# Summing part of the modulation on VectorE during the merge of the branches, in a two-layer hybrid backbone on one core

## The reference

```python
sh1, sc1, g1, sh2, sc2, g2 = split(silu_c @ w_mod[l] + b_mod[l], 6)   # c_ctx the same: csh1 ...
u = h * (1 + sc1) + sh1
p = u @ w_in[l]                       # conv, attention, mLSTM inputs, and 3 x 1024 branch gates
y = (sig(ga)*(ya @ w_a) + sig(gb)*(yb @ w_b) + sig(gc)*(yc @ w_c)) @ w_out
h = layer_norm(alpha*h + g1*y);  u2 = h * (1 + sc2) + sh2
h = layer_norm(alpha*h + g2*moe(u2))  # 16 experts, top 1 group, top 2 experts in it
```

## Time and profile before

| what | us |
| --- | --- |
| median of 3 runs (lowest, highest) | 1658.95 (1657.82, 1660.44) |
| the profiled execution, its own time | 1658.97 |
| its span, first to last instruction | 1657.1 |
| TensorE busy | 1561.0 (94%) |
| VectorE busy | 768.3 (46%) |
| ScalarE busy | 374.5 (23%) |
| GpSimd busy | 219.1 (13%) |
| transfers, mean | 220 GB/s |
| granted TensorE clock, mean | 0.981 of full |

### The profile page before, as it was taken

How to read it: one execution, slowest core, us unless ns; L and a number is a source line. 1 busy time by engine, 2 the same in 40 slices (tenths; PEclk the granted TensorE clock), 3 DMA queues, 4 the chain that set the end, 5 groups by cost and what they waited for, 6 DMA issues and landing times.

```text
span 1657.1 us, 32449 instructions
## 1 busy us (share of the span) xinstructions
PE 1561.0 (94%) x13532; PEld 981.8 (59%) x13532; DVE 768.3 (46%) x1543; ACT 374.5 (23%) x894; POOL 219.1 (13%) x239
## 2 busy tenths in 40 slices
PE   6999999999999999999999896999999998999974
PEld 3454475465444468656566454767688887555532
DVE  3169825475001023653336536395553125565455
ACT  1100036642000010422222122002742002212111
POOL 0200000000000000033334230000000000543421
PEclk9999999999999999999999997999999998999997
DMA  9534647602313242699669998452215467999993
GB/s 334 172 106 138 228 159 272 200 22 81 113 52 114 64 152 74 253 406 406 250 251 404 406 400 300 152 143 80 64 42 191 154 216 260 374 407 407 407 408 152
DMA packets 175107, 365.30 MB, mean 220 GB/s; under 512 B 14337, under 2 KB 93801, under 8 KB 174451
## 3 DMA queue, kind: packets, MB, share of 16 engines
q1 hardware_dynamic: 162400, 330.43, 54.9%
q0 software_dynamic: 10112, 27.06, 4.8%
q10 hardware_dynamic: 2451, 5.73, 1.1%
HBM read 356.66 MB, written 10.62 MB: 222 GB/s over the span
## 4 chain that ended last, share of the span: by engine, by line
PE 64%; DVE 5%; SPq 4%; DMA 3%; ACT 2%; issue 1%; POOL 0%; DVEq 0%; POOLq 0%; ACTq 0%
PE psum L1120 62%; SPq L930 4%; PE psum L1658 1%; DMA yab<-in_moe_w_gu 1%; DMA uT<-in_moe_w_gu 1%; PE psum L1410 0%; DMA convT<-us,x_row 0%; DMA yab<-ys 0%; PE psum L1228 0%; DMA ys<-qkT,y_row 0%; DVE st L2153 0%; DVE H L2725 0%; DVE st L2154 0%; DVE H L2166 0%; PE psum L1551 0%
## 5 line engine op out<-in xcount | busy, mean ns | idle before, releaser
L1120 PE MATMUL psum<-uT,ring 128*128 128x512 f32 (+1 forms) x1440 | 494.7, 501 | 2.9 <-ACT uT L1823 2.1
L1120 PEld LDWEIGHTS psum<-uT,ring 128*128 128x128 f32 x1440 | 272.9, 191 | 212.0 <-issue 192.3
L1120 PE MATMUL psum<-ring,mo_tok 128*32 128x256 f32 x4992 | 317.0, 382 | 20.3 <-DVE ring L2702 19.0
L1120 PEld LDWEIGHTS psum<-ring,mo_tok 128*32 128x32 f32 x4992 | 153.7, 110 | 129.9 <-DVE ring L2702 35.5
L1120 PE MATMUL psum<-ring,v_tok 128*32 128x256 f32 x2496 | 150.7, 382 | 0.5 <-ACT v_tok L2072 0.5
L2310 DVE SCALAR_TENSOR_TENSOR convT<-upad,cwT,convT 128x512 f32<-128x512 f32 (+1 forms) x240 | 132.4, 614 | 2.1
L1120 PEld LDWEIGHTS psum<-ring,v_tok 128*32 128x32 f32 x2496 | 82.2, 111 | 54.8 <-issue 1.8
L1120 PE MATMUL psum<-ring,uT 128*128 128x256 f32 (+1 forms) x576 | 113.6, 357 | 0.0
L1120 PEld LDWEIGHTS psum<-ring,uT 128*128 128x128 f32 x576 | 99.1, 190 | 16.6 <-issue 5.4
L2527 DVE TENSOR_TENSOR arena<-psum,mqk 128x512 f32<-128x512 f32 (+1 forms) x16 | 8.9, 558 | 206.2 <-PE psum L1120 206.2
L2702 DVE COPY ring<-uT 128x1024 f32<-128x1024 f32 x73 | 49.8, 728 | 83.8 <-PE psum L1120 76.0
(11 more groups left out here) (361 smaller groups left out, 1547.7 us busy)
## 6 DMA issues: line engine op xcount, KB each, us to landing
ring<-in_w_in SPq DMA_DIRECT2D x104, 512.0 KB, 4.8
ring<-in_w_mod SPq DMA_DIRECT2D x84, 512.0 KB, 7.3
yab<-in_moe_w_gu SPq DMA_DIRECT2D x51, 512.0 KB
arena<-in_moe_w_gu SPq DMA_DIRECT2D x47, 512.0 KB
uT<-in_moe_w_gu SPq DMA_DIRECT2D x47, 512.0 KB
mv_tok<-in_moe_w_gu SPq DMA_DIRECT2D x26, 512.0 KB
uT<-in_moe_w_dn SPq DMA_DIRECT2D x26, 512.0 KB
mqk<-in_moe_w_gu SPq DMA_DIRECT2D x25, 512.0 KB
```

The source lines that it names most:

```text
L1120: return nc.tensor.matmul(dst, lhsT, rhs, start=start, stop=stop)
```

## The change

The units of `w_mod` are grouped anew. Group 2 becomes six units of the first layer (twelve halves), which take the place of the old group 3 in the attention's steps; the eight spots behind mqk, mv and mo are gone. Groups 3, 4 and 5 become one group of 14 units, 28 halves: the two units of the first layer's last gate and all of the second layer. These are not multiplied on TensorE. VectorE multiplies each 128x512 piece of a half by the matching column of `cT` (one scalar for each partition) and adds it up in one of eight 128x512 buffers, one for each unit and stream: for six units both streams, for the other eight the latent stream alone, 20 sums. TensorE then only adds the 128 partitions, four sums at a time in the four column groups, with a stationary operand that is one column of ones (`add_partitions`).

In the stream, eight halves follow the weights of each pair of merge steps, four for each step, 28 in all; VectorE sums four halves after it has merged a step, and a slot is freed when its half is summed. The loads at the border, the wait on `mod_used` before the last gathers, and the column steps of the old groups 2, 4 and 5 fall away; the column step of the new group stands after the second output product. `cT` gets narrower (its width follows the largest group computed on TensorE).

```diff
+    [(0, u) for u in range(4, 10)],
+    [(0, 10), (0, 11)] + [(1, u) for u in range(12)],
 ]
+SUMMED = 3
+BOTH_STREAMS = [(0, 10), (0, 11)] + [(1, u) for u in range(4)]
+SUMS = [(x, c) for x in MOD_GROUPS[SUMMED] for c in range(2 if x in BOTH_STREAMS else 1)]
+SUM_BUFS = 8
+SUM_BATCH = 4
+HALVES_PER_MERGE = 4
+BATCH_AFTER_MERGE = {1: 0, 2: 1, 3: 2, 5: 3}
...
                 if c + l + 1 < KD // 2:
                     used_gates(c + l + 1)
+                for j in (2 * c, 2 * c + 1):
+                    used_sums(halves_at_merge(l, j))
...
+                def add_partitions(batch):
+
+                    sums = SUMS[SUM_BATCH * batch:SUM_BATCH * (batch + 1)]
+                    pe.wait_ge(summed, 2 * MOD_GROUPS[SUMMED].index(sums[-1][0]) + 2)
...
+                    for q, (x, c) in enumerate(sums):
+                        row = 2 * MOD_GROUPS[SUMMED].index(x) + c
+                        last = mm(psum[MOD_BANK][32 * q:32 * q + 32, :], one_column[:, 31 - row:63 - row],
+                                  sum_bufs[sum_of(x, c) % SUM_BUFS], batch == 0, batch == N_BATCHES - 1)
+                    last.then_inc(mod_used, 1)
...
                     if j + GATES_AHEAD[l] < KD:
                         branch_gates(j + GATES_AHEAD[l])
+                    if l == 0 and j in BATCH_AFTER_MERGE:
+                        add_partitions(BATCH_AFTER_MERGE[j])
...
+                    if key == out_keys(0)[0]:
+                        add_partitions(N_BATCHES - 1)
+                    if key == out_keys(0)[1]:
+                        modulation_columns(SUMMED)
...
-                    for t in range(2):
+                    for t in range(nt):
                         gather_tile(t)
                     act.wait_ge(rows_used, 2 * l + 2)
                     gate_rows(1)
-                    act.wait_ge(mod_used, halves_to(5))
-                    for t in range(2, nt):
-                        gather_tile(t)
-                    keep_rows(5)
...
+                def sum_half(x):
+
+                    m, u, half = x
+                    streams = [c for y, c in SUMS if y == (m, u)]
+                    wait_slot(dve, "mod", *x)
...
+                    for q in range(4):
+                        for c in streams:
+                            acc = sum_bufs[sum_of((m, u), c) % SUM_BUFS]
+                            w, scale = slot_wide(slot_of("mod", *x))[:, q, :], cT[:, 4 * half + q, MOD_AT + c:MOD_AT + c + 1]
+                            if (half, q) == (0, 0):
+                                last = v.tensor_scalar(acc, w, scale, None, ALU.mult)
+                            else:
+                                last = v.scalar_tensor_tensor(acc, w, scale, acc, ALU.mult, ALU.add)
+                        if q < 3:
+                            link(last)
+                    last.then_inc(summed, 1)
...
+                    for x in halves_at_merge(l, j):
+                        sum_half(x)
```

More of the change, by code:

```diff
@@ L103, in halves_to, with mod_uses, gate_group, halves_at_merge @@
     return sum(len(halves) for halves in MOD_HALVES[:g + 1])
[L106 to L125, removed]
+def mod_uses(g):
+    return halves_to(min(g, SUMMED - 1)) + (N_BATCHES if g == SUMMED else 0)
+def gate_group(layer, which):
+    return 2 if (layer, which) == (0, 0) else SUMMED
+MOD_STEPS = (1, 2, 3, 4, 5, 6, 7, 9, 11, 13, 15, 17)
+MOD_SPREAD = dict(zip(MOD_STEPS, MOD_HALVES[2]))
+assert len(MOD_STEPS) == len(MOD_HALVES[2])
+COLUMNS_UNIT = len(UNITS)
+def halves_at_merge(layer, j):
+    return MOD_HALVES[SUMMED][HALVES_PER_MERGE * j:HALVES_PER_MERGE * (j + 1)] if layer == 0 else []
+assert sum(len(halves_at_merge(0, j)) for j in range(KD)) == len(MOD_HALVES[SUMMED])
+def sum_of(x, c):
+    return SUMS.index((x, c))
 BRANCHES = ("bga", "bgb", "bgc")
@@ L581, in build @@
         sig = mqk
+        sum_bufs = [buf[:, x * 512:(x + 1) * 512] for buf in (ln_rows, convT[:, :, :].rearrange("p a b -> p (a b)"))
+                    for x in range(SUM_BUFS // 2)]
         spread_rows = [[qkT[:, 4, :], qkT[:, 5, :], upad_flat[:, 3 * T:4 * T]],
@@ L740, in used_modulation, with used_sums @@
                 stream.append((("mod",) + x, mod_used, MOD_ORDER.index(x) + 1))
-            def used_pair(pair):
-                for x in pair:
-                    used_modulation(x)
+            def used_sums(halves):
+                for x in halves:
+                    stream.append((("mod",) + x, summed, MOD_HALVES[SUMMED].index(x) + 1))
             def used_gates(c):
@@ L972, in _ @@
                     at += NS
-                    for x in range(len(BORDER) if l == 0 else 0):
-                        load_border(x)
                 else:
@@ L1414, in _ @@
                         outputs_of_group(i // 2 - 2)
-                    modulation_pair(mod_at(l, "step", i))
+                    if l == 0 and i in MOD_SPREAD:
+                        modulation(MOD_SPREAD[i])
                     spread_gates("step", i)
-                    if l == 0 and i == COLUMNS_STEP:
-                        modulation_columns(2)
                 pe.wait_ge(gate_em, l + 1)
@@ L1594, in _ @@
                 done(last, "count", l)
-                if l == 0:
-                    for x in MOD_HALVES[4][1:]:
-                        modulation(x)
                 def uses_until(key):
@@ L1748, in _ @@
                     gate_rows(1, G2)
-                    for x in BORDER:
-                        modulation(x)
                 else:
@@ L2560, in _ @@
                         norm_half(1, part)
+                    if key == out_keys(0)[1]:
+                        modulation(SUMMED)
+                        wait_drained(dve, "modt", SUMMED)
+                        for w in (2, 3):
+                            fold_norm(w)
                 modulate(1)
```

138 lines of the change are left out of this document (44 added, 94 removed).

## The result

The changed kernel took **1700.99 us** (median of 4 runs, 1697.62 to 1703.95), beside 1659.7 us for the kernel before: a ratio of 1.0258, 95% interval 1.0238 to 1.0277. Forecast were 1690 us and a range of 1674 to 1704. The profiled execution was the slowest of the four: 1703.95 us, span 1702.2 us, 45.1 us above the span before.

What follows compares the result with a forecast made beforehand. TensorE, busy for 94% of the span, was taken to bound the kernel. Gains of 21.7 us against losses of 52.8 us, net +31.1 on 1658.97 us, gave 1690 us; the range was 1674 to 1704 us.

Steps and rivals of the forecast that it cites:

- The gaps' place and cause: Merge stretch: TensorE idles after steps 1, 3 and 5, since the next a/b weights queue behind halves in the ring; 38.4 us.
- VectorE's own term: Sums on VectorE: 160 added operations, some 111 us, with VectorE's capacity not the problem.
- Their size: Merge stretch: three gaps of 12.8 us each, a batch of 1.0 us inside each, 38.4 us lost in all.
- At 30.9 us TensorE is ready for step 2: Merge, counted from step 1's start: a/b weights end a burst of eight transfers, 4.19 MB, 12.7 us; TensorE resumes 12.8 late.
- The clock: Behind each of three merge gaps TensorE restarts at half clock, losing 2.7 us: 8.1 us in all, bounds 0 and 10.
- Rival B: Merge stretch: the gaps come without the clock's loss, 1682 us in all; chance 0.10.
- Batches and column step: Added on TensorE: batches of four matmuls at 1.0 us, two outside the gaps (2.0 us), and a column step of 1.0.
- The output wait: After the merge: the output product waits for VectorE to merge step 7, 2.3 us lost, between 0 and 5.
- Before the merge: Up to the merge: eight pairs gone from TensorE gain 16.4 us, the attention's wait and column step 1.8 us.
- Routing: Six halves gone around the routing gain nothing; the gathering product may start at half clock: 1.0 us lost, between 0 and 2.7.
- The border: Between the layers: six halves and their 6 MB of loads gone, scatter and gather freed: 2.5 us gained, bounds 0 and 6.
- rival C: Merge gaps: the burst moves at 278 GB/s, 16.7 us in all, three times 4.0 us more, 1702 us; chance 0.12.

Runs made afterwards that it cites:

- again: The changed kernel run and profiled a second time, nothing changed: 1701.26 us, ratio 1.025 to the kernel before; its profiled execution took 1697.12 us.

## Why the prediction was right, and where its terms were off

- **The gaps' place and cause: right.** Three, before steps 2, 4 and 6, each begun by a burst of six transfers of halves and the a, b weights when the third gate product ends. Taking loads out from ahead of these weights, with c's wait at its own product, closes them; taking VectorE's work out doesn't. VectorE's own term was right too: it is busy for 110.5 us more than before, for 111.
- **Their size: 46.7 us where 38.4 were forecast.** Two parts. The burst was read to the end of its bytes, 12.7 us; to its landing the same rows give up to 14.5, and the three gaps show 13.8 to 14.2 (462.37 less 448.4 in the first). That is 1.2 us a gap. And the step "At 30.9 us TensorE is ready for step 2. Its weights were issued last of a burst of four slots" left out that TensorE waits for the branch c weights in the same place: 1.6 us a gap. 3 x (1.2 + 1.6) = 8.4 of 8.3 us. Idle spans of 14.3 to 14.7 us in place of 11 to 12 are also what the prediction listed as a sign that its burst was mis-sized.
- **The clock: 6.4 us (again: 6.9) where 8.1 were forecast.** 9.00, 9.53 and 8.91 us, each less 7.03. The Trainium skill's rule on oscillation ("TensorE: Matmul & The Clock Gate", HAM oscillation), weighed in the prediction, holds here in all six gaps of the two profiles (granted clock 0.55 and 0.50 in windows behind the first). Rival B is out.
- **Batches and column step: right**, 1.06 us each and 0.97 us. The output wait was 3.39 us for 2.3, with a slower product behind it in one profile of two.
- **Before the merge: 14.1 us gained in the profile, 17.1 in "again", for 18.2.** Nine of the eleven profiles with the pairs moved or gone reach the merge at 382.7 to 384.1 us; the two at 386 have the slow product near 70 us, which the change doesn't touch.
- **Routing: 1.0 us of loss forecast, 2.0 and 0.4 measured.** Its parts differ from the forecast's. The gathering product paid its half clock in full (9.56 less 7.41 = 2.15 us), not beside VectorE. Against that, 0.65 us were gained behind it, where the column step stood, which the prediction had put at nothing; and in "again" the product also started 1.1 us sooner in its stage. The first gathered tokens were late by 1.6 to 2.3 us more than before, which the prediction didn't have.
- **The border: 5.0 us gained for 2.5.** The scatter lost its excess, as said; the gather was taken to keep "most of its time" and lost 1.8. The stage of the experts and the border is still only 2.1 to 2.5 us shorter, since the late tokens lie in it: there the forecast came out by two misses that cancel.
- **The sum:** against "again" (1697.12 us, 38.2 above 1658.97) the forecast of +31.1 is short by 7.1 us: 7.0 more in the merge (of it gaps 7.7, clock -1.2), 1.5 in the output products, 1.1 before the merge, less 0.2 in the stages up to the second layer's merge and 2.3 behind its start. The last has no term and no run explains it. The median, 1700.99 us, is 11 us above the forecast; the profile of 1703.95 us lost its further 6.9 us outside the merge.
- **The range was partly luck.** Its upper end, 1704 us, came from rival C, which named nearly the right time for the wrong reason: the rate was 350 to 400 GB/s, not 278. The forecast's own terms had no room for a burst read to its landing and a second wait behind it.

## What to carry to other kernels

Where weights pass through a ring in order, new loads cost what they put ahead of the next needed weights: count the slots between the last release and that load, and read a burst to its landing, not to its last byte. Before pricing a gap, look at every wait that stands at its end, and give each operand its wait at its first use. Work moved to an idle engine pays if its operands fit into the slack of the transfers; sixteen of the 28 halves, four in a cycle, gained 13 us here, and all of them, eight in a cycle ahead of the next weights, lost 41.

## What was not expected of the hardware

- The same product near 70 us took 20.87 us in the eleven profiles in which it waited 0.63 to 1.74 us for its transfer, and 22.56 us in the two in which it waited 2.53 and 2.85 us. The granted clock was 0.68 in 70 to 75 us in the changed kernel's slower profile and 1.00 in "again". Yet one wait of 2.19 us cost nothing, waits of 2.6 to 2.8 us halved the clock three times out of three, and one of 3.39 us did so in three profiles of six.
- The last of eight transfers issued in a run (b) landed 9.9 to 10.4 us after its issue in the changed kernel, against 4.4 to 5.8 us in the run with only the first halves. Issuing a and b took SyncE 0.50 and 1.07 us in such a burst, 0.37 and 0.51 us without one.
- The same burst landed up to 1.3 us later in some gaps than in others, with TensorE at work and without. What makes the difference stays open.
